# A trunk layer's output weights kept split in a scratch, the second gate folded into w_ff2, and other orders at the seams

## The reference, cut to what matters

```
sh1, sc1, g1, sh2, sc2, g2 = split(silu(c) @ w_ada + b_ada)      # one vector each
proj = (rms_norm(x, norm1_g) * (1 + sc1) + sh1) @ w_in
mix  = concat(attention, conformer conv, gated conv, pooling)(proj) @ w_out
x    = x + g1 * mix
h    = rms_norm(x, norm2_g) * (1 + sc2) + sh2
x    = x + g2 * (square(relu(h @ w_ff1)) @ w_ff2)
```

## Time and profile before

| what | value |
|---|---|
| three runs | 2329.91 to 2335.45 us, median 2334.64 |
| profiled execution | 2330.76 us |
| its span, first to last instruction | 2329.0 us |
| mean granted TensorE clock | 0.984 |
| busy: TensorE / its weight loads | 2211.4 / 1858.8 us |
| busy: VectorE / ScalarE / GpSimd | 1836.4 / 1120.6 / 358.5 us |
| moved by DMA | 311.54 MB, mean 134 GB/s |

### The profile page before, as it was taken

One profiled execution on the slowest core, in us unless ns is written; L12 is line 12 of the kernel. 1 busy time (PEld: TensorE's weight loads), 2 busy tenths in 40 slices (PEclk: granted clock), 3 DMA queues, 4 the chain that ended last, 5 costly groups with the idle time before them and its releaser, 6 DMA issues. The chain is left out here.

```text
span 2329.0 us, 29748 instructions
## 1 busy us (share of the span) xinstructions
PE 2211.4 (95%) x11258; PEld 1858.8 (80%) x11258; DVE 1836.4 (79%) x2587; ACT 1120.6 (48%) x1787; POOL 358.5 (15%) x285
## 2 busy tenths in 40 slices
PE   7999999987999999999999999988999999999996
PEld 4987897767889888778888788867878888888885
DVE  6548796889989876777668988878687777888886
ACT  4531545458988854433335454523443333554540
POOL 0442044824355630000000000000000000000000
PEclk9999999989999999999999999999999999999998
DMA  7441534130000054244447444345244444644333
GB/s 271 154 158 55 166 111 140 50 96 28 15 10 24 11 174 150 70 151 152 154 155 261 155 139 167 136 172 199 90 140 154 150 151 153 239 171 168 134 132 144
DMA packets 168522, 311.54 MB, mean 134 GB/s; under 512 B 10664, under 2 KB 82620, under 8 KB 167356
## 3 DMA queue, kind: packets, MB, share of 16 engines
q1 hardware_dynamic: 168292, 309.60, 39.0%
q10 hardware_dynamic: 88, 0.04, 0.0%
HBM read 219.42 MB, written 90.18 MB: 133 GB/s over the span
## 5 line engine op out<-in xcount | busy, mean ns | idle before, releaser
L2912 PE MATMUL ps<-sb_h_hi 128*128 128x512 f32 x512 | 202.8, 396 | 25.2 <-DVE sb_out L2336 21.4
L2914 PE MATMUL ps<-sb_h_hi,sb_h_lo 128*128 128x512 f32 x512 | 201.8, 394 | 0.0
L2913 PE MATMUL ps<-sb_h_lo,sb_h_hi 128*128 128x512 f32 x512 | 201.8, 394 | 0.0
L2559 PE MATMUL ps<-sb_h_hi,sb_w_hi 128*128 128x512 f32 x448 | 177.7, 397 | 0.8 <-DVE sb_w_lo L2188 0.8
L2876 PE MATMUL ps<-sb_h_hi,sb_w_hi 128*128 128x512 f32 x448 | 174.9, 390 | 1.4 <-ACT sb_u_full L1578 1.4
L2561 PE MATMUL ps<-sb_h_hi,sb_w_lo 128*128 128x512 f32 x448 | 174.7, 390 | 0.0
L2560 PE MATMUL ps<-sb_h_lo,sb_w_hi 128*128 128x512 f32 x448 | 174.6, 390 | 0.0
L2877 PE MATMUL ps<-sb_h_lo,sb_w_hi 128*128 128x512 f32 x448 | 174.6, 390 | 0.0
L2912 PE MATMUL ps<-sb_w_hi 128*128 128x512 f32 x384 | 149.7, 390 | 0.0
L2913 PE MATMUL ps<-sb_w_lo,sb_w_hi 128*128 128x512 f32 x384 | 149.6, 390 | 0.0
L2914 PE MATMUL ps<-sb_w_hi,sb_w_lo 128*128 128x512 f32 x384 | 149.6, 390 | 0.0
(11 more groups left out here) (341 smaller groups left out, 5902.8 us busy)
## 6 DMA issues: line engine op xcount, KB each, us to landing
left_scratch<-sb_u_sum SPq DMA_DIRECT2D x128, 256.0 KB, 6.4
sb_right<-in_w_ff SPq DMA_DIRECT2D x16, 2048.0 KB, 8.6
sb_h_lo_full<-left_scratch SPq DMA_DIRECT2D x64, 512.0 KB, 3.7
sb_w_full<-in_w_ff SPq DMA_DIRECT2D x28, 1024.0 KB, 6.3
left_scratch<-sb_u_full SPq DMA_DIRECT2D x96, 256.0 KB, 2.0
sb_w_full<-left_scratch SPq DMA_DIRECT2D x48, 512.0 KB, 3.2
sb_w_raw<-in_w_in SPq DMA_DIRECT2D x16, 1024.0 KB, 5.6
sb_ada<-in_w_ada SPq DMA_DIRECT2D x32, 512.0 KB, 5.2
```

Source lines behind the costliest of these rows:

```text
L2559: M(dst, ah, bh, start=(n == 0), stop=False)
L2912: M(dst, hi[:, k, tok], hi[:, 2 + k, :], start=fresh and k == 0, stop=False, skip_group_check=True)
L2913: M(dst, hi[:, k, tok], low[:, 2 + k, :], start=False, stop=False, skip_group_check=True)
L2914: ins = M(dst, low[:, k, tok], hi[:, 2 + k, :], start=False, stop=k == 1, skip_group_check=True)
```

## The change

1. In the first half, the high and low parts of w_out are stored in a scratch (8 stores of 1 MB, in tiles 3 to 6 of the output projection). At the handover to the second half they are loaded from there (`reload_w_out`) in place of loading w_out and splitting it.
2. In the fast groups 2 to 14 of the first half, VectorE multiplies w_ff2 by gate g2 in place (`fold`), piece by piece: 3 x 512 and 2 x 512 columns per group, each loaded, multiplied and stored to a second scratch, from which `load_right` then reads in both halves. The gate multiplications at the end of each half are gone.
3. In the last chunk VectorE evacuates slot 1 first and adds sums to the late rows afterwards; the last results are added to the rows straight from PSUM; part 5 is added to the rows by itself.
4. In chunk 0 the evacuations of slots 3 and 4 come earlier in VectorE's list.
5. The w_ff1 load of group 3 is issued once the plain products are done, ahead of a store; TensorE no longer waits for the last plain `relu` before group 2 (ScalarE does, before the seed); and in group 2 ScalarE's `w1_head(g + 1, 0)` comes after the reseed.

```diff
+FOLDS = FAST - 1
+FOLDED = ([(3 * i, min(3, 20 - 3 * i), 0) for i in range(7)] + [(3 * i, 3, 1) for i in range(6)],
+          [(20 + 2 * i, 2, 0) for i in range(6)] + [(18 + 2 * i, 2, 1) for i in range(7)])
...
             def load_right(c):
-                sp.dma_start(right[:, :, :], w_ff2_v[:, 4 * c:4 * c + 4, :]).then_inc(right_ld, 16)
+                sp.dma_start(right[:, :, :], w_gated_v[:, 4 * c:4 * c + 4, :]).then_inc(right_ld, 16)
...
+            def load_fold(b, k):
+                if k:
+                    sp.wait_ge(fold_st[b], fold_no(k))
+                sp.dma_start(fold_tile(b, k), fold_rows(w_ff2_v, b, k)).then_inc(fold_ld[b], 16)
+
+            def store_fold(b, k):
+                sp.wait_ge(folded, 2 * k + b + 1)
+                sp.dma_start(fold_rows(w_gated_v, b, k), fold_tile(b, k)).then_inc(fold_st[b], 16)
...
+                    if hc == 0 and 3 <= t < 3 + KC_OUT:
+                        store_w_out(t - 3)
...
+                    if g == PLAIN - 1:
+                        sp.wait_ge(ff1_mm, 4 * PLAIN * (hc + 1))
+                        load_w1(hc, PLAIN + 1)
                     store_left_u(hc, g, 6, 4)
...
                     store_left_sums(hc, g - 1)
+                    if hc == 0 and k:
+                        store_fold(1, k - 1)
                     if g > PLAIN:
                         store_left_u(hc, g - 1, 5, 4)
                     store_left_sum4(hc, g - 1)
+                    if folds:
+                        if k == 0:
+                            sp.wait_ge(t_lo, 4)
+                        load_fold(0, k)
...
+                    if folds:
+                        load_fold(1, k)
                     store_left_u(hc, g, 6, 2)
+                    if folds:
+                        store_fold(0, k)
...
                 if hc == 0:
+                    sp.wait_ge(wo_st, 2 * 16 * KC_OUT)
                     sp.wait_ge(part_mm, part_no(G, 1, 3))
-                    load_w_out(1, 0)
+                    reload_w_out(0, 0)
+                    reload_w_out(0, 1)
...
                     sp.wait_ge(part_mm, part_no(G, 3, 3))
-                    load_w_out(1, 1)
+                    reload_w_out(1, 0)
+                    reload_w_out(1, 1)
                     sp.wait_ge(upper_done, 1)
-                    load_w_out(1, 3)
+                    reload_w_out(3, 1)
                     sp.wait_ge(part_mm, part_no(G, 5, 3))
-                    load_w_out(1, 2)
+                    reload_w_out(2, 0)
+                    reload_w_out(2, 1)
+                    sp.wait_ge(upper_done, 1)
+                    reload_w_out(3, 0)
...
                     A(u_part[:, :], psum[:, 2, :], ACT.Copy).then_inc(copied, 1)
-                    if not last:
+                    if PLAIN < g and not last:
                         w1_head(g + 1, 0)
                     act.wait_ge(fast_mm, SLOTS * n + 3)
                     A(psum[:, 3, :], psum[:, 1, :], ACT.Copy).then_inc(reseeded, 1)
+                    if g == PLAIN:
+                        w1_head(g + 1, 0)
...
+                def fold(b, g):
+                    k = g - PLAIN
+                    if hc == 0 and k < FOLDS:
+                        y, (_, n, a) = fold_tile(b, k), FOLDED[b][k]
+                        dve.wait_ge(fold_ld[b], fold_no(k + 1))
+                        V.tensor_tensor(out=y, in0=y, in1=gate_row[:, 1:2, a * BLK:(a + 1) * BLK].to_broadcast([P, n, BLK]),
+                                        op=ALU.mult).then_inc(folded, 1)
...
                         for i in range(3, 5):
                             w1_tail(g + 1, i)
+                    fold(0, g)
                     dve.wait_ge(fast_mm, SLOTS * n + 5)
...
                     u_sums(g)
+                    fold(1, g)
...
+                def finish(s, p, rows_no, added):
+
+                    dve.wait_ge(part_mm, part_no(chunk_no(hc, c), order_of(c).index(s), 2 * p + 1))
+                    dve.wait_ge(dve_chain, added)
+                    add_to_rows(rows_no, 1, two(side_of(s), p)).then_inc(part_read, 1)
...
                 tails(c, 6)
-                for p in range(2):
-                    scaled(6, p, 0)
                 evacuate(c, 1, 0)
-                for p in range(2):
-                    add_to_rows(2 + p, 0, sum_of(6, p))
                 evacuate(c, 1, 1)
-                for p in range(2):
-                    scaled(1, p, 0)
+                dve.wait_ge(part_read, read_no(hc, c, 1, 1))
+                add_to_rows(0, 0, sum_of(1, 0))
                 evacuate(c, 5, 0)
+                add_to_rows(1, 0, sum_of(1, 1))
                 evacuate(c, 5, 1)
+                added = mark(add_to_rows(0, 1, sum_of(3, 0)))
+                add_to_rows(1, 1, sum_of(3, 1)).then_inc(upper_done, 1)
                 dve.wait_ge(part_read, read_no(hc, c, 5, 1))
...
+                dve.wait_ge(dve_chain, added)
+                top = [mark(add_to_rows(0, 1, sum_of(5, 0)))]
+                dve.wait_ge(upper_done, hc + 1)
+                top.append(mark(add_to_rows(1, 1, sum_of(5, 1))))
+                added = mark(add_to_rows(2, 1, sum_of(4, 0)))
+                first = [mark(add_to_rows(2 + p, 0, sum_of(6, p))) for p in range(2)]
+                dve.wait_ge(dve_chain, added)
+                bottom = mark(add_to_rows(2, 1, sum_of(5, 0)))
+                finish(3, 0, 0, top[0])
+                finish(3, 1, 1, top[1])
+                finish(4, 0, 2, bottom)
+                link(add_to_rows(3, 1, sum_of(4, 1)))
+                bottom = mark(add_to_rows(3, 1, sum_of(5, 1)))
+                finish(4, 1, 3, bottom)
+                for t in range(4):
+                    dve.wait_ge(part_mm, part_no(chunk_no(hc, c), SLOTS - 1, t))
+                    dve.wait_ge(dve_chain, first[t // 2])
+                    row = x_late(4 + t)[:, 0:BLK]
+                    ins = V.tensor_tensor(out=row, in0=row, in1=psum[:, 4 + t, :], op=ALU.add)
+                    if t % 2:
+                        ins.then_inc(part_read, 1)
```

More of the change, by code:

```diff
@@ L560, in wo_loaded, with wo_parts @@
         def wo_loaded(hc, i):
-            return wo_ld[i], (32 if i > 1 else 16) + 16 * hc
+            return wo_ld[i], (32 if i > 1 else 16) + 32 * hc
+        def wo_parts(hc, i):
+            return [(wo_d[(2 * i + m) * P:(2 * i + m + 1) * P, :], f32(part))
+                    for m, part in enumerate((wo_hi(hc, i), wo_lo(hc, i)))]
         def quarter(part, kb, b):
@@ L799, in _, with load_w_out, store_w_out, reload_w_out @@
             sp.wait_ge(h_ready, NT)
-            def load_w_out(hc, i):
-                if hc == 0 and i == 0:
+            def load_w_out(i):
+                if i == 0:
                     raw_free(2 * NI)
-                if hc == 0 and i > 1:
+                if i > 1:
                     for a in range(2):
-                        sp.dma_start(wo_raw(0, i)[:, 2 * a:2 * a + 2, :],
+                        sp.dma_start(wo_raw(i)[:, 2 * a:2 * a + 2, :],
                                      w_out_v[:, 2 * i + a, :].rearrange("p (c n) -> p c n", n=BLK)).then_inc(wo_ld[i], 16)
                     return
-                sp.dma_start(by_k2(wo_raw(hc, i)), w_out_v[:, 2 * i:2 * i + 2, :]).then_inc(wo_loaded(hc, i)[0], 16)
+                sp.dma_start(by_k2(wo_raw(i)), w_out_v[:, 2 * i:2 * i + 2, :]).then_inc(wo_ld[i], 16)
+            def store_w_out(i):
+                for rows, part in wo_parts(0, i):
+                    sp.dma_start(rows, part).then_inc(wo_st, 16)
+            def reload_w_out(i, m):
+                rows, part = wo_parts(1, i)[m]
+                sp.dma_start(part, rows).then_inc(wo_ld[i], 16)
             def load_mix(n):
@@ L948, in _ @@
                             load_left(hc, 0, s)
+                    k, folds = g - PLAIN, hc == 0 and g < FG - 1
                     store_left_sums(hc, g - 1)
+                    if hc == 0 and k:
+                        store_fold(1, k - 1)
                     if g > PLAIN:
@@ L1445, in att_root, with wo_head @@
                 A(ams[:, 16:32], ams[:, 0:16], ACT.Sqrt, bias=eps_col, scale=1.0 / VD).then_inc(arms_ready, 1)
-            def wo_head(hc, i, before=None):
-                act.wait_ge(*wo_loaded(hc, i))
-                if before is not None:
-                    act.wait_ge(*before)
-                hi = wo_hi(hc, i)
-                A(by_k4(hi) if hc == 0 and i > 1 else hi, wo_raw(hc, i), ACT.Copy).then_inc(whi_ready, 1)
+            def wo_head(i, before):
+                act.wait_ge(*wo_loaded(0, i))
+                act.wait_ge(*before)
+                hi = wo_hi(0, i)
+                A(by_k4(hi) if i > 1 else hi, wo_raw(i), ACT.Copy).then_inc(whi_ready, 1)
             def mix_head(n):
@@ L2119, in first_guess, with wo_tail @@
                 V.tensor_scalar(guess, guess, -1, ROOT_BITS, ALU.mult, ALU.add).then_inc(arms_ready, 1)
-            def wo_tail(hc, i):
-                dve.wait_ge(whi_ready, wo_no(hc, i) + 1)
-                hi, low = wo_hi(hc, i), wo_lo(hc, i)
```

(22 more changed lines are left out.)

133 lines of the change are left out of this document (53 added, 80 removed).

## The result

Five runs of the changed kernel took 2302.65 to 2313.33 us, median 2309.22; five of the kernel before on the same chip 2329.91 to 2335.45, median 2330.29. The ratio is 0.9898, 95% interval 0.9875 to 0.9921: 21 us gained. The forecast was 2300.5 us, and its sum on the profiled execution 34.2 us gained. The profiled execution of the changed kernel took 2309.22 us; its span is 2307.4 us against 2329.0, 21.6 us less.

A forecast was written before the change was run, and what follows sets the result against it. TensorE, busy 95% of the span, bounds it; the gain is its waits on VectorE. 20 + 17 + 1 - 1.3 - 1.5 - 1 = 34.2 us off 2330.76, plus 3.9, gave 2300.5; range 2293 to 2311.

The forecast's parts named there:

- rival (a): Steady groups, first half: fold store delays w1, TensorE waits 0.6 to 1 us per group; 2307 to 2312; chance 0.14.
- The end of the second half: Last chunk to span end: evacuations ahead of late rows, scalings and products removed, last rows stored together; 20 us gained.
- the handover to its first matmul: First half's last chunk to out-projection: w_out parts reloaded, VectorE owes only mix_tail, TensorE starts earlier; 16.6 us gained.
- The predicted new wait of 1.0 us before slot 6: Last chunk: the second evacuation of slot 4 ends at 1561.5, where slot 6 wants it at 1560.7.
- the 2.3 us of idle before the out-projection: Handover: TensorE would start the out-projection at 1566.75 after 2.3 us idle, behind VectorE's mix_tail.
- The first also waits for its load ... has 8 us to land and takes 3 to 4.: Steady groups, first half: the first fold's load lands in time; the groups lose 1 us in twelve.
- 1.3 us lost: Group 2, first half: slots 0 to 5 run unstalled, then a sum22 wait and clock fall; 1.3 us lost.
- 1.5 was foretold: Group 2, second half: slot 6 starts unchanged after a single 3.4 us wait; 1.5 us lost, 0 to 2.
- the next tile runs 0.7 us behind: Out-projection, second half: x row 0 lands about 1578, transposes want its tile at 1584; next tile 0.7 us behind.
- in place of +1: Handover clock: loss taken as 1 us after 2.3 us idle, where before had 2; 1 us gained.
- Rival (b): Handover: queue at 365 GB/s is the bound, item 2 and x row 0 late; 17 becomes 9.6, 2308; chance 0.11.
- 0.5 us gained per half: First chunk: earlier evacuations of slots 3 and 4 remove a 1.21 us wait; next chunk's slot 0 1.0 us late.

The follow-up runs named there:

- experiment 4: Changed kernel with the adds of late rows 4 to 7 put back between the two evacuations of slot 1 in each half's last chunk; 2332.16 us, ratio 1.0004.
- experiment 8: Kernel before with only the two adds into late rows 4 to 7 moved behind the evacuations of slot 3; 2314.68 us, ratio 0.9914.
- experiment 1: Changed kernel with the first fold of each steady first-half group moved behind the sum into block 22 and its square; 2297.87 us, ratio 0.9846.
- 6: Changed kernel without any folds: chunks read w_ff2 directly, so the second gate is missing from the computation; 2297.72 us, ratio 0.9839.
- 7: Kernel of experiment 1 with the first groups' order put back as in the kernel before; 2302.95 us, ratio 0.9863.
- 3: Changed kernel with stores of output rows 0 and 1 ahead of three w_out reloads, and the third mixed tile's load ahead of the x-row wait; 2306.05 us, ratio 0.9878.
- 12: Changed kernel with only the third mixed tile's load issued ahead of the wait for the second half's first x rows; 2306.85 us, ratio 0.9893.
- experiment 2: Changed kernel with chunk 1's last left tile loaded ahead of chunk 2's right parts in each half; 2305.07 us, ratio 0.9876.
- 5: Changed kernel with the edits of experiment 1, experiment 2 and 3 together; 2293.47 us, ratio 0.9823.
- 9: Kernel of 5 with, in group 2, five low parts of w1 moved behind the sum, and the first-half fold behind them; 2289.33 us, ratio 0.9805.
- experiment 11: Kernel of 10 with the very first fold behind the sum into block 12 and its store behind group 4's w1 load; 2283.09 us, ratio 0.9791.
- 10: Kernel of 9 with slot 5's first evacuation in chunk 0 two VectorE steps earlier; 2287.40 us, ratio 0.98.

## Why the prediction was right, and where its terms were off

**The total.** The measured 2309.22 us lies in the stated range of 2293 to 2311, but not in the forecast's own 2296 to 2306, and of the 34.2 us summed up 21.6 came. It is in the range because rival (a) had widened it. The forecast also stood 3.9 us nearer to the result than its sum, as it added the distance of the three runs' median from the profiled execution; the median of the five runs with the result, 2330.29, is 0.5 below that execution. Both are luck.

**The end of the second half (20 us, measured 19.7) and the handover to its first matmul (16.6, measured 16.1).** The mechanism was right: VectorE's order held the evacuation behind late rows. It is shown from both sides, by putting the wait back (experiment 4) and by moving it alone (experiment 8). The predicted new wait of 1.0 us before slot 6 is there as 0.8, the 2.3 us of idle before the out-projection as 1.92. But the text gave the gain to the whole rewriting, "Removed: eight scalings and the four products"; by experiment 4 some 24 of 36 us are the order, and the other 11 to 12 us the rest of the rewriting together.

**"The first also waits for its load ... has 8 us to land and takes 3 to 4."** This step failed. It is the second fold's load of 512 KB that takes some 4 us. The first's, of 768 KB, takes 7.0 in the median and up to 10.0 (the row of these loads, and the line of `load_fold`, L909 of the changed kernel, for both sizes):

```profile
sb_w_gated<-in_w_ff SPq DMA_DIRECT2D x12, 768.0 KB, 7.0
...
DMA to landing us min/median/max: 3.7/4.7/10.0
```

The load for the fold at 1024.45 was issued at 1014.47, behind six stores and with w1's last packets. The window from 1015 to 1025 below has the queue in use all the time at 341 GB/s. A slack of 0.2 us did not bear it. The forecast looked for the danger in w1 (rival (a), whose range of 2307 to 2312 holds the result by accident) and not in the fold's own load.

**"1.3 us lost" in group 2.** Right, and by its own terms. The sum had slot 6 start 0.75 us nearer and 2 us lost behind its wait; measured are 0.5 and 1.7, and the wait before the sum, foretold as 4.7 us, is 4.73. Without the fold ahead of the sum slot 6 starts 2.4 us nearer (experiment 1), which is the forecast's figure less its 1.7 us for the fold, and the clock does not fall: the stretch gains 2.3 us (experiments 1 and 6), 1.7 of them by the new order (7), and the fold there costs 3.5. So the whole loss in this half is the price of one fold's place in VectorE's list; the forecast did not draw that from its own terms. In the second half 1.5 was foretold and 1.1 measured, but of the eight profiled runs with this code, all with a wait of 2.75 us, four gained 0.5 and four lost 1.0 to 1.1. What decides is the clock (below).

**"the next tile runs 0.7 us behind".** This term was mis-sized: 5.6 us. The queue was not slower than the 415 GB/s assumed, and what the sum counted came about in time: against tile 0's first matmul the last part of w_out landed after 6.3 us (5.8 foretold) and the first x row after 12.4 (11.3). (The bytes listed, at 415 GB/s from 1536.3, give 1569 for the last part and not the 1572.5 written; the measured time bears out the written one.) What the sum had nowhere is the load of the third mixed tile, which stood behind the x rows in SyncE's program, though every queue entry past which a wait is put counts. With that load moved, 0.7 us are lost, the figure of the forecast (experiments 3 and 12), so the missing 4.9 us are this load's. The clock's +2.5 us in place of +1 is luck: behind the same wait of 1.9 us it fell in experiments 3 and 12, and tile 0 gave 0.9 to 1.0 us there. In windows of the changed kernel (TensorE busy, its clock, the queue's share and rate):

```profile
1550.00:1558.00 8.00, 8.00 (x37) 1.00 1.03 429
1558.00:1562.00 4.00, 4.00 (x19) 1.00 1.13 315
1562.00:1582.00 20.00, 17.05 (x72) 1.00 1.01 415
1577.00:1582.00 5.00, 5.00 (x23) 1.00 1.01 412
1582.00:1588.00 6.00, 6.00 (x28) 1.00 0.52 135
1015.00:1025.00 10.00, 10.00 (x45) 1.00 1.04 341
```

Rival (b) priced this stage at 365 GB/s; the windows refute that (406 over the 32 us from 1550 to 1582, the slow 4 us in them included). The Trainium skill, "DMA: Bandwidth & Descriptors", section "Where 436 GB/s comes from", bounds transfers between HBM and SBUF at about 358 GB/s; this trace disagrees, with 429 for loads and 412 over the last 5 us to 1582, when stores of rows were moved beside the last parts of w_out.

**"0.5 us gained per half" in the first chunks.** It was 0.1 lost and 3.6 lost. The wait of 1.21 us did go, the one on the part copy came as foretold (1.2 for 1.0), but the left tile behind the 2 MB load was missing from the argument (experiment 2). Of the 3.6 us, at least 1.9 belong to this one execution, as the other runs show.

Of the signs named ahead, the wait for late rows under 2.5 us (2.15), the seam, the last matmul to the end in 5 us (5.6) and the wait on the sum in group 2 (4.73, and 2.75 for 3) came. One failed: groups 3 to 14 at 19.0 us, which took 19.4 on average.

## What to carry to other kernels

Ask first of an in-order engine whether something late stands ahead of something wanted: two moved lines gave 20 us, about as much as the whole rewriting. Where work is tucked into an engine's idle time, put it behind the operation that others wait for and check the landing time of its own load, at its own size and under that stage's traffic, slowest case included. Where a queue's program gets a wait, list every load behind it; a forecast whose total falls into its range, as this one's did, still needs its terms measured one by one.

## What the runs showed of the hardware

The same wait does not always cost the same. Eight kernels have TensorE idle for 2.75 us, waiting on the same sum in group 2 of the second half. In the changed kernel and in experiments 3, 5 and 12 the stretch cost about 1.5 us more than in 1, 2, 4 and 6. The granted clock was 0.66 to 0.67 over the 5 us behind the wait in the four dear ones, and 1.00 in the four cheap ones. First the changed kernel, then experiment 1, each from the wait's end:

```profile
1738.00:1743.00 5.00, 4.76 (x14) 0.66 0.16 57
```

```profile
1730.00:1735.00 5.00, 4.85 (x21) 1.00 0.28 81
```

Fourteen matmuls, part of them at the 1.2 GHz level (the clock was 0.50 from 1740 to 1742), and 21 at 2.4: 7 x 5/21 = 1.7 us. A wait of this length is a risk of 1.6 us beside its own 2.75, and none of these runs says what decides it.

A shorter wait does the same. Ahead of the second half's out-projection TensorE is idle for 1.91 or 1.92 us in all twelve kernels with the new handover. In eight of the profiled executions (experiments 1, 3, 5, 6, 7, 9, 11, 12) the clock was 0.66 over the 5 us behind it and tile 0 took 12.6 us; in four (the changed kernel, 2, 4, 10) it was 1.00, and tile 0 took 11.0 to 11.5. The forecast had taken half a fall here, since in the kernel before the clock fell behind 2.48 us and not behind 1.99; in these executions it comes whole or not at all. The kernel of experiment 11, which still has this wait but none longer from 840 us on, varied least: 2282.74 to 2283.76 us in five runs.

The rate also went with the packets: from 1558 to 1562, when 1903 of 1940 packets were under 2 KB (the mixed tiles' 512-byte rows), the queue carried 315 GB/s at full use, where the rows of x and of w_out's parts, 4 and 8 KB long, went at 412 to 429. No run changes the packets alone.
